# Output projection in column-tile pairs with seven half products, its operands made slice by slice in branch B

## The reference

```python
h = rmsnorm(x, norm_g)
proj = jnp.einsum('bld,dp->blp', h, w_in)        # gates, short conv, GLA inputs
branch_a = jnp.einsum('blc,cd->bld', za, w_branch_a)
branch_b = jnp.einsum('blv,vd->bld', zb, w_branch_b)
merged = jax.nn.sigmoid(ga) * branch_a + jax.nn.sigmoid(gb) * branch_b
x = x + jnp.einsum('bld,de->ble', merged, w_out)  # the output projection
y = rmsnorm(x, final_norm_g)
```

## Time and profile before

| | us |
|---|---|
| median of three runs | 2525.13 (2524.56 to 2528.24) |
| the profiled execution | 2524.39 |
| its span, first to last instruction | 2522.6 |
| PE busy in the span | 2481.6 (98%) |
| DVE busy | 1789.8 (71%) |
| ACT busy | 1066.5 (42%) |
| output projection, PE idle before it to the last copy | 2284.5 to 2500.1 |

### The profile page before, as it was taken

The page is one execution under the profiler, slowest core; times in us unless marked ns, Lnnn a source line. Parts: engine busy times, 40 slices in busy tenths (PEclk is TensorE's granted clock), DMA queues, the critical chain, the costliest instruction groups (busy, mean ns, idle before and its releaser), DMA issues.

```text
span 2522.6 us, 44420 instructions
## 1 busy us (share of the span) xinstructions
PE 2481.6 (98%) x18531; PEld 2436.4 (97%) x18531; DVE 1789.8 (71%) x2536; ACT 1066.5 (42%) x1557; POOL 216.1 (9%) x369
## 2 busy tenths in 40 slices
PE   8999999999999999999999999999999999999996
PEld 7999999999999999999999999999999999999996
DVE  7458667585688788787787888876668778785223
ACT  5343344443544443443444444444455445334222
POOL 2002012020110000000000011100000101111000
PEclk9999999999999999999999999999999999999998
DMA  6315335253453434433443445654569769557232
GB/s 181 84 52 169 109 99 162 57 185 90 130 154 102 117 101 117 111 88 104 117 117 101 110 124 166 178 143 129 176 188 290 226 199 288 148 165 217 83 83 75
DMA packets 443662, 349.24 MB, mean 138 GB/s; under 512 B 13813, under 2 KB 416673, under 8 KB 439617
## 3 DMA queue, kind: packets, MB, share of 16 engines
q1 hardware_dynamic: 412418, 230.65, 33.2%
q0 software_dynamic: 31056, 115.91, 13.8%
HBM read 276.60 MB, written 69.91 MB: 137 GB/s over the span
## 4 chain that ended last, share of the span: by engine, by line
PE 92%; DVE 4%; DMA 2%; ACT 1%; issue 1%; ACTq 0%; SPq 0%; POOL 0%; DVEq 0%
PE bank L1580 32%; PE acc L1580 25%; PE acc L1498 19%; PE acc L421 6%; PE acc L1396 2%; PE acc L1454 1%; PE bank L1424 1%; DMA raw<-in_w_out 1%; PE bank L1451 1%; PE bank L1448 1%; DMA y_f<-zt_d 1%; PE bank L1428 1%; PE acc L1597 1%; DMA x_rows<-in_x_prompt 0%; DVE act_x L2302 0%
## 5 line engine op out<-in xcount | busy, mean ns | idle before, releaser
L1744 DVE TENSOR_TENSOR ring_lo<-pa,ring_hi 128x1024 fp32r<-128x1024 f32 x476 | 581.3, 1221 | 187.4 <-ACT ring_hi L917 184.9
L917 ACT ACTIVATE ring_hi<-pa 128x1024 fp32r<-128x1024 f32 x476 | 502.6, 1056 | 363.0 <-PE bank L1580 207.0
L1498 PE MATMUL acc<-act_y,w_hi 128*128 128x288 f32 x2560 | 520.1, 298 | 0.0
L1580 PE MATMUL bank<-act_x,ring_hi 128*128 128x288 f32 x2240 | 439.0, 294 | 0.8 <-ACT act_x L1202 0.6
L1580 PE MATMUL bank<-act_y,ring_hi 128*128 128x288 f32 x2112 | 415.0, 295 | 0.2 <-DVE act_y L2346 0.2
L1498 PEld LDWEIGHTS acc<-act_y,w_hi 128*128 128x128 f32 x2560 | 410.2, 189 | 4.0 <-issue 1.2
L1580 PE MATMUL acc<-act_x,ring_hi 128*128 128x288 f32 x1984 | 396.4, 294 | 1.3 <-DVE ring_lo L1744 1.3
L1498 PE MATMUL acc<-act_y,w_lo 128*128 128x288 f32 x1280 | 377.9, 295 | 0.0
L1580 PEld LDWEIGHTS bank<-act_x,ring_hi 128*128 128x128 f32 x2240 | 357.4, 189 | 1.3 <-ACT act_x L1202 0.8
L1580 PEld LDWEIGHTS bank<-act_y,ring_hi 128*128 128x128 f32 x2112 | 335.7, 189 | 0.6 <-DVE act_y L2346 0.4
L1580 PEld LDWEIGHTS acc<-act_x,ring_hi 128*128 128x128 f32 x1984 | 320.0, 189 | 1.5 <-issue 1.5
(11 more groups left out here) (326 smaller groups left out, 3177.2 us busy)
## 6 DMA issues: line engine op xcount, KB each, us to landing
pa<-in_w_in SPq DMA_DIRECT2D x208, 512.0 KB, 5.2
raw<-in_w_in SPq DMA_DIRECT2D x40, 1024.0 KB, 5.7
states<-in_state_gla POOLq DMA_DIRECT2D x64, 256.0 KB, 3.1
out<-states POOLq DMA_DIRECT2D x64, 256.0 KB, 3.3
pa<-in_w_branch_a SPq DMA_DIRECT2D x32, 512.0 KB, 5.9
pa<-in_w_branch_b SPq DMA_DIRECT2D x32, 512.0 KB, 5.0
raw<-in_w_out SPq DMA_DIRECT2D x16, 1024.0 KB, 5.7
gate_tile<-gate_d POOLq DMA_DIRECT2D x32, 288.0 KB, 3.4
```

Source lines behind the costliest of these rows:

```text
L917: A(ring_hi[g % RING][:, :], piece_of[src][u % 2][:, :], ACT.Copy).then_inc(part_hi, 1)
L1498: mm = nc.tensor.matmul(half_bank[h % 2][:, 0:HALF], (w_hi, w_lo)[a][par][:, k * P:(k + 1) * P], y_of(k, b, j), start=(k == 0 and n == 0), ...
L1580: mm = nc.tensor.matmul(out, (ring_hi, ring_lo)[a][r][:, k * P:(k + 1) * P], slot_of(slot, b)[:, k, :], start=(p in (0, 1, 3) and k == 0 a ...
L1744: V.tensor_tensor(ring_lo[g % RING][:, :], piece_of[SOURCE[p]][u % 2][:, :], ring_hi[g % RING][:, :].bitcast(F32), ALU.subtract).then_inc( ...
```

## The change

**The output projection becomes eight pairs.** `PAIR_C` follows `PAIR_B`; w_out is read as pairs of neighbouring channel tiles (`w_o_h`, the two halves of the input channels are the even and the odd tiles), so one branch B pair m gives slice m of all seven operands. `channel_unit`, `last_unit`, `merged_hi`, `merged_lo` and the loops over units are gone.

```diff
+C_SPLITS = ((2, 3, 0, 4, 7), (4, 4, 1, 0, 7), (5, 5, 0, 7, 8), (6, 6, 2, 0, 7), (6, 7, 1, 7, 8), (6, 7, 2, 7, 8),
+            (8, 8, 3, 0, 8), (8, 8, 4, 7, 8), (8, 9, 6, 7, 8), (10, 10, 5, 0, 8))
...
-    w_o_k = w_out[0].rearrange("(k p) c -> p k c", p=P)
+    w_o_h = w_out[0].rearrange("(k h p) c -> h p k c", h=2, p=P)
...
             def branch_b(u, p):
...
-                    V.tensor_tensor(merged_of(t)[:, 1, :], quarter(mix_tile, 0, 1), v_2[:, :], ALU.add
-                                    ).then_inc(mixed[0], 1)
+                    V.tensor_tensor(b12, b12, v_2[:, :], ALU.add).then_inc(mixed[0], 1)
+                    dve.wait_ge(mixed[0], PAIRS_B + m + 1)
+                    dve.wait_ge(c22_read, u + 1)
...
+                    link(V.tensor_tensor(t1, b11, b12, ALU.subtract))
...
+                    V.tensor_tensor(t3, b22, b12, ALU.subtract)
+                    V.scalar_tensor_tensor(out=t2, in0=b22, scalar=-1.0, in1=t1, op0=ALU.mult, op1=ALU.subtract
+                                           ).then_inc(c_made, 1)
                 if p == 6:
...
+                    V.scalar_tensor_tensor(out=t4, in0=t2, scalar=-1.0, in1=b21, op0=ALU.mult, op1=ALU.subtract
+                                           ).then_inc(c_made, 1)
```

**In branch B**, DVE makes t1, t3, t2 (p = 5) and t4 (p = 6) of the slice; ACT and DVE split t3 and t4 (`slice_hi`, `slice_lo`), and the b11 of the first four pairs (`MADE`). POOL stores the slices in DRAM (`zw_d` raw, `zp_d` split), and only then reloads the tiles of gate and branch A, which the split parts lay in:

```diff
+                pool.wait_ge(c_made, 2 * m + 1)
+                pool.dma_start(zw_d[0:3, :, m, :].rearrange("q p t -> p q t"), y_f32[:, KH + 4:KH + 7, 0, HALF:T]
+                               ).then_inc(way_out, 16)
+                pool.wait_ge(t_lo, 2 * m + 1)
...
+                pool.wait_ge(t_lo, 2 * m + 2)
+                pool.dma_start(zp_d[1, 0, :, m, :], high_at(6).bitcast(F32)).then_inc(t4_out, 16)
+                pool.dma_start(zp_d[1, 1, :, m, :], low_at(6).bitcast(F32)).then_inc(t4_out, 16)
                 for n in range(2):
-                    t, following = 2 * B_PAIRS[m] + n, 2 * B_PAIRS[m + 1] + n
-                    pool.wait_ge(mixed[n], PAIRS_B + m + 1)
-                    load_gate(1, following)
...
+                    pool.wait_ge((t3_out, t4_out)[n], 32 * (m + 1))
+                    load_gate(1, 2 * m + 2 + n)
                     pool.wait_ge(ma_out[n], 16 * (PAIRS_B - 1))
-                    pool.dma_start(mix_tile[:, n, :], ma_d[following]).then_inc(ma_in[n], 16)
+                    pool.dma_start(mix_tile[:, n, :], ma_d[2 * m + 2 + n]).then_inc(ma_in[n], 16)
```

More of the change, by code:

```diff
@@ L461, in c12_done, with kind_of @@
         def c12_done(u):
+            if u >= PAIR_C:
+                return c12_read, u + 1 - 2 * PAIRS_B
             return (c12_read, u + 1) if u < PAIR_A else (mixed[0], u + 1 - PAIR_A)
-        by_act = [u < PAIR_A and FIRST[u][0] in ("c", "ga", "gb") for u in range(NPAIR)]
+        def kind_of(u):
+            return FIRST[u][0] if u < PAIR_A else "branch" if u < PAIR_C else "out"
+        by_act = [kind_of(u) in ("c", "ga", "gb", "out") for u in range(NPAIR)]
         def c21_done(u):
-            if u >= PAIR_A:
+            if PAIR_A <= u < PAIR_C:
                 return mixed[1], u + 1 - PAIR_A
@@ new lines, in squares @@
+            def squares(m, tiles, n0, n1, group, count):
+                act.wait_ge(squared, count)
+                junk = mix[(PAIR_C + min(m, PAIRS_O - 2)) % 2][:, :, :].rearrange("p a t -> p (a t)")
+                w = (n1 - n0) * P
+                for t in tiles:
+                    dst = junk[:, t * 2 * P:t * 2 * P + w] if t < NT else square_b[:, 0:w]
+                    ins = A(dst, rows_of(m, [t], n0, n1)[:, 0, :], ACT.Square,
+                            accum_out=parts[:, group * (NT + 1) + t:group * (NT + 1) + t + 1])
+                ins.then_inc(squared, 1)
@@ L1172, in _ @@
                         save(u, 1, v_3, 4)
+                    if p == 0 and last == "out":
+                        save_c21(u - 1)
                     if p == 0 and last == "c":
@@ new lines, in _ @@
+                    if 0 < m < PAIRS_B and p == 0:
+                        slice_hi(u - 1, 6)
+                    for n, c in enumerate(C_SPLITS):
+                        if g - (PAIR_C - 1) * NPROD == c[0]:
+                            rest_hi(n)
+                    if u == PAIR_C and p == 2:
+                        A(stat[:, 40:41], eps[:, :], ACT.Sqrt)
+                    if u > PAIR_C and p == 5:
+                        act.wait_ge(out_sum, 2 * (u - PAIR_C))
+                        squares(u - 1 - PAIR_C, range(NT + 1), 0, 2, u - 1 - PAIR_C, u - 1 - PAIR_C)
@@ L2261, in branch_b @@
             def branch_b(u, p):
-                m, t = u - PAIR_B, 2 * B_PAIRS[u - PAIR_B]
+                m = u - PAIR_B
                 b1, b2, b3 = psum_of(u)
+                b11 = e1[:, :] if m == PAIRS_B - 1 else made_at(m, 0)
+                b12, b21, b22 = quarter(mix_tile, 0, 1), made_at(m, 3), made_at(m, 5)
+                t1, t2, t3, t4 = (made_at(m, q) for q in (1, 2, 4, 6))
                 if p in (3, 4):
@@ new lines, in _ @@
+                    if 0 < m < PAIRS_B and p == 0:
+                        slice_lo(u - 1, 4)
+                    if 0 < m < PAIRS_B and p == 1:
+                        slice_lo(u - 1, 6)
+                    for n, c in enumerate(C_SPLITS):
+                        if g - (PAIR_C - 1) * NPROD == c[1]:
+                            rest_lo(n)
+                    m = u - 1 - PAIR_C
+                    if m >= 0 and p in (1, 3):
+                        add_rows(m, p // 2)
+                    if m >= 0 and p == 6:
+                        weight(m, range(NT + 1), m + 1)
```

602 lines of the change are left out of this document (318 added, 284 removed).

## The result

| | before | changed |
|---|---|---|
| median of 14 runs, us | 2525.64 (2523.67 to 2531.00) | 2531.41 (2527.80 to 2534.58) |
| ratio, 95% interval | | 1.0020 (1.0012 to 1.0027) |
| the profiled execution | 2524.39 | 2530.43 |
| its span | 2522.6 | 2528.7 |

The change makes the kernel slower, by 0.20%, which is little but clear of the noise. The forecast was 2513 with a range of 2498 to 2523: the sign is wrong, and the range is missed by 8 us.

The account below looks back on a forecast made before the run. TensorE, busy 98% of the span, was taken to bound the kernel. Terms -29.3 + 1.4 + 5 + 9.3 + 1.5 = -12.1 from the median of 2525.13 gave 2513 us, range 2498 to 2523.

Parts of the forecast that it names:

- The projection: Output projection: 8 pairs of 168 matmuls replace 16 units of 96, 186.3 us against 215.6, so -29.3 us.
- Start of branch B: First pair of branch B: VectorE's inserted t1, t3 and t2 show there, +1.4 us (0 to 3).
- POOL's round trip: Branch B: reloads wait for the stores of t3 and t4; +0.7 us for each of 7 pairs, 5 us (0 to 12).
- "Only one half tile has to wait": Branch B: argument against the rival that POOL's round trip sets the pace with 2 us lost per pair.
- The change to phase C: Change from branch B: late raw operand, then a VectorE chain with nothing in parallel; +9.3 us in several waits (1.7 to 12).
- The tail: After the last copy: half a MB more late rows and runs of 1 KB for 8 KB; +1.5 us (-1.5 to +5).
- VectorE's work on the rows of phase C: Phase C pairs: 3 operations in place of 11, two adds and a weighting; 2.8 us against 5.4 dropped, no wait expected.
- The second: Rival: POOL's round trip sets branch B's pace, stores at 4.2 us, 2 us lost in each of 7 pairs, 2526; chance 0.12.
- The third: Rival: TensorE's clock falls to 1.2 GHz at the phase change; above 2530, with 7 products 2535; chance 0.06.
- the signs of being wrong: Branch B at 22.2 a pair, a change under 4 us, a clock below 1.00 before the end, or waits inside phase C.

Follow-up runs that it names:

- e5: e2 with t1, t3 and t2 of pairs 0 to 6 issued behind the split of the next pair's second product on VectorE; 2515.04 us.
- e2: Changed kernel with t3 and t4 parts kept elsewhere, gate and branch A tiles reloaded ahead of the stores, b11 slices split at the phase change; 2514.72 us.
- e13: Changed kernel with SP's four weight pieces in branch B held until POOL's reloads of half 0 or half 1 have landed; 2519.30 us, ratio 0.9965.
- e4: Changed kernel with POOL asking for half 0's reload once t3's stores landed, ahead of the wait for t4's low part; 2554.63 us, ratio 1.0116.
- e11: e8 with output rows laid out so that six of the last eight parts go out in runs of 3 KB; 2509.67 us, ratio 0.9934.
- e10: Changed kernel with t1, t3 and t2 of pairs 0 to 6 behind the split on VectorE, nothing else; 2535.62 us, ratio 1.0044.
- e8: e2 with e5's order, b11 slices rounded one offset later, and operand 1's last slice split ahead of operand 2's first seven; 2510.30 us.
- e12: e11 with each third of a scaled output row stored as soon as it is scaled; 2508.41 us, ratio 0.9929.

## Why the prediction was wrong

**The projection, -29.3: right.** -28.0 by the copies; the pairs of w_out are 23.33 us apart, as stated, and nothing waits inside phase C.

**Start of branch B, +1.4 (0 to 3): +2.9 by the first copies, +1.2 by the third,** which follow TensorE: right. VectorE's three inserted operations explain about 0.6 of it (e5). The rest was not taken apart; it is not the round trip, since e2 has it too.

**POOL's round trip, +5 (0 to 12): +17.4. This step failed.** The mechanism was named, and its pieces on VectorE were right: from the operations at p = 4 to the low part of t4 I had 14.8 us, the chain shows 14.2 to 14.6. The stores were taken too long (3.5 us, by the chain 2.0 to 3.0) and the reloads far too short: 3.3 from the earlier trace rows, where they measured 5.5 and 6.1 (medians) and the one that closes the loop 6.6 on the mean. The earlier trace rows came from a moment in the pair when SP asked for nothing. The change moved the reloads behind the stores, and there they met the weight pieces, 512 KB each, three asked for beside them and the fourth before the last had landed. I followed the time at which POOL asks, and did not ask what else is on the transfer engines then. e13 undoes most of that and gives back 12 us by the medians, 9.6 of it in the six pairs by the traces. The sum had also put the loop against a pair that starts on time, with 0.35 us of cover; in a loop there is none, each us of each piece counts in each pair (e4 above all). Its pieces as predicted, 14.8 on VectorE, 4.1 for the stores and 4.3 for the reloads with their issues, are 23.2 us, 1.0 and not 0.7 above a pair. "Only one half tile has to wait" was wrong as well: VectorE waited 16.2 us in six pairs for half 0 and 10.5 for half 1. That didn't add to the time, since the chain runs through half 1 alone.

```profile
DVE part L2360 <- DMA mix_tile<-ma_d: 16.2, 6, 3.1
...
DVE part L2366 <- DMA mix_tile<-ma_d: 10.5, 6, 2.6
```

**The change to phase C, +9.3: +9.0 by the first copies, +10.2 by the second, and partly for other reasons.** TensorE's waits there are 6.7 us where 9 were expected, and 2.7 are the clock's (below). The chain on VectorE is the predicted one, and its end, the low part of t1 for product 1, was TensorE's longest wait (3.1). But the raw operand landed in 5.0 us, not 7.7, so ScalarE rounded it early and the copy of `part_81` held nobody up. The chain started late because VectorE waited for the last reload of half 0 instead. The mistakes cancelled: that the number fits is luck.

```profile
2301.16 1.89 ACT L1250 ACTIVATE act_x<-x_f 128x2016 fp32r<-128x2016 f32 x1 [0.94 <-DMA x_f<-zw_d]
2302.95 0.39 ACT L1195 ACTIVATE part<-acc 128x288 f32<-128x288 f32 x1
```

**The tail, +1.5 (-1.5 to +5): -0.1** in all; in it half of the short runs cost 0.8 at most (e11).

**A sum beside these.** VectorE's work on the rows of phase C was set against 5.4 us dropped. That is all eleven operations; eight go, 3.9 us by the 0.49 of a linked one. 2.8 is still less, and nothing waited there.

**The rivals.** The second, that the round trip sets the pace of branch B, was what happened, at a chance of 0.12 and with 2 us a pair; it is 2.9 for each of six. Its price came from longer stores, which did not occur. Its time, 2526, was 5 short.

The third, a fall of the clock at the change, occurred too, in a small form. Windows of the changed kernel at the change (columns as above):

```profile
2316.00:2318.00 2.00, 1.54 (x11) 1.30 (x10) 2.00 (x3) 1.95 (x3) 0.00 (x0) 0.93 1.09 276
2318.00:2320.00 2.00, 1.09 (x5) 0.74 (x4) 1.97 (x3) 0.35 (x1) 0.00 (x0) 0.50 1.18 382
2320.00:2322.00 2.00, 0.00 (x0) 0.00 (x0) 1.97 (x4) 1.23 (x1) 0.00 (x0) 0.50 1.01 421
...
2326.00:2328.00 2.00, 2.00 (x10) 2.00 (x10) 2.00 (x3) 1.48 (x2) 0.00 (x0) 0.51 1.03 376
2328.00:2330.00 2.00, 2.00 (x17) 2.00 (x17) 2.00 (x3) 0.61 (x2) 0.41 (x1) 1.00 1.08 391
```

After three waits of 1.2, 1.3 and 0.5 us the clock goes to half (1.2 GHz), stays there over the wait of 3.1, and is full again just before 2328; 10 records in 2 us stand against 17. The 24 matmuls from the end of the last wait, 2322.23, to 2328.07 take 5.8 us where 24 take 3.17 at full clock: 2.7 lost, on one product and not on seven. That the clock fell below 1.00 ahead of the end is one of the signs of being wrong that the prediction named. The Trainium skill's warning in "TensorE: Matmul & The Clock Gate", HAM oscillation, agrees with these rows: the waits between matmuls cost more than themselves. Shorter spells, of 3.4 to 7 us, stand once in branch B of the changed kernel (2184 to 2188), six times in e4 and three times in e10, whose pairs are the longest, never in the first two profiles of the kernel before from 2090 to 2290, and not in e8 or e12 there. In branch B no matmul lies in the chain, so it cost nothing there that shows.

The largest error was the size of one term: 17.4 lies outside POOL's own range of 0 to 12, because both ends of it rested on the length of the stores and none on that of the reloads. Of the 18 us between the forecast and the median, 13 are in the terms from B0 on (-12.1 against +1.1), 12 of them in this one; the rest lies ahead of B0, where the prediction had no term.

## What to carry to other kernels

The length of a transfer from a trace holds for the moment it was read at: when a change moves it, ask what the other queues have on the transfer engines at its new place. When a wait closes a loop from one iteration to the next (load, work, store, load), sum the loop by itself and compare it with the iteration; slack inside the iteration doesn't cover anything in it. A buffer lent to another use for half an iteration is paid for with such a loop; here other places and a reload at its old time were worth 17 us, and holding back a transfer that was not urgent 12.
